# The reciprocal norm of layer 1's projections, multiplied by GpSimd and not by VectorE

## The chip, the cores and the metric

The program runs on one core of one Trainium2 chip. The metric is the device time of one execution in microseconds (us); the time of a kernel is the median of its runs. Engines are named as the profile names them: PE is TensorE, PEld its weight load, DVE is VectorE, ACT is ScalarE, POOL is GpSimd, SP is SyncE. Each runs its own list of instructions in order, and engines wait for one another through semaphores alone.

## What is computed

A two-layer trunk over 256 frames of width 2048, in float32. Layer 0 is attention beside a convolution module, layer 1 is a gated DeltaNet; behind each stands a SwiGLU feed-forward. The change lies in layer 1:

```python
def gated_deltanet_mixer(h, w_in, short_conv, a_log, dt_bias, o_norm, w_out):
    proj = h @ w_in                       # h is rms_norm(x, g): x * rsqrt(mean(x*x) + eps) * g
    qkv, z, b_logit, a_logit = jnp.split(proj, splits, axis=-1)
    qkv = jax.nn.silu(causal_depthwise_conv(qkv, short_conv))      # width 4
    q, k, v = jnp.split(qkv, [GDN_QK_WIDTH, 2 * GDN_QK_WIDTH], axis=-1)
    ...                                   # l2-normalise q and k, beta, log-decay g per head
    o = chunk_gated_delta_rule(q, k, v, g, beta)
    o = rms_norm(o, o_norm) * jax.nn.silu(zf)
    return o.reshape(bsz, seq, GDN_V_WIDTH).astype(h.dtype) @ w_out
```

The reciprocal norm of a frame is the same for all columns of the projection, so the kernel multiplies by it behind the matmul and not ahead of it.

## The kernel before

**Groups and chunks.** Every projection is cut into groups of 512 output columns, held transposed (128 columns on the partitions, 4 tiles of them, 256 frames along the row). A group goes through its 2048 input rows in 4 chunks `c`. SP loads a chunk of weights (1 MB) into `raw`; ACT rounds it into `w_hi` (L556, two halves), DVE makes the rest `w_lo` (L902, two halves), and PE multiplies both (L1664 and L1657) into the accumulators `acc`. At the end of a group ACT copies one half of `acc` into `tmp` (L563) and DVE adds the other (L908, 4 instructions) into `ut`; the last of the 4 gives the semaphore `acc_free` the value 4G+4, G being the number of the group.

**What follows a group.** A group is finished inside the next one, in `post`. DVE multiplies `ut` (128x1024) by `rstd`, the reciprocal norm (L967), and tells so by `scaled`. For a group of q, k or v DVE then runs the short convolution (L992, 4 instructions with one weight, then L994, 12 more), and ACT applies silu (L721). For a group of z, ACT applies silu to `ut` directly. The next group's sums on DVE wait until that silu has read `ut`.

**Segments of layer 1.** `in1_first` has the 4 groups q, k, v0, v1 of head set 0. `in1` runs three times; round j has z0 and z1 of set j and q, k, v0, v1 of set j+1, and beside them the delta rule of set j. `in1_last` has z0 and z1 of set 3, the delta rule of set 3 and 4 groups of the output projection (kind `resid`), whose inputs come back from DRAM (`og_save`). The multiplications at hand are those of the groups whose kind begins with gdn: 4 + 18 + 2 = 24.

**The delta rule** is a generator per engine (`gdn_pe`, `gdn_dve`, `gdn_act`, `gdn_pool`), advanced by ticks between the instructions of the groups; a tick lets it go on to the next `yield`, so the order on an engine is fixed when the program is built. POOL's part of set j, in its order: load `L` and `I` from `g_rows` (L1507), clear `XT`, add masks to `L` and `I` (L1512, L1514, 2 instructions each over 128x1024), clear `Xb` and `XTb`, then 8 small DMAs `l_diag` and 2 DMAs `Lb` (L1528, L1532), all inside the visit of z0; in the visit of q `x_diag` and `XT` (L1537, L1544); at the end of the round `og_save` (L1549) and a wait until it has landed. ACT needs the masks for its exponentials (L841), DVE needs `Lb` for an inversion of small triangles (L1419 to L1492), which keeps it busy through most of the group z1. The l2 norm of q and k is multiplied in by DVE at L1321, after the convolution of the v1 ahead has been started, and PE's first product of the delta rule (L1776) waits for it.

**In `in1_last`** POOL loads the first half of an old output back into `qk_in` (L532) at its visit of the first output group (b == 2), and the second half (L537) once two pieces of the first are used. ACT (L586) and DVE (L975) split them into `xs`, which PE needs for the group.

POOL comes to `post(before)` at the very start of a visit, ahead of the ticks of that visit:

```python
            def visit(here, before, kc):
                ...
                if before is not None:
                    post(before)
                ...
                if s.name == "in1_first" and b == 3:
                    ...                       # g_rows out, then wait until they have landed
                if s.deltanet:
                    if b == 0:
                        steps[0] = gdn_pool(pool, set_of(here))
                    if s.name == "in1_last" and b == 2:
                        ...                   # L532: qk_in<-og_save
```

Of the kernel before, what the change touches and what calls it, by code (L numbers as in the profile page):

```python
# [9 lines left out]
ALU = mybir.AluOpType  # L10
# [3 lines left out]
P = 128  # L14
T = 256
# [28 lines left out]
class Group:  # L44


    def __init__(self, w, col, rhs, kind, kc=4, row=0, step=0, at=0, norm=None):
        self.w, self.col, self.rhs, self.kind = w, col, rhs, kind
        self.kc, self.row, self.step, self.at, self.norm = kc, row, step, at, norm


class Segment:


    def __init__(self, name, n, groups, deltanet=False):
        self.name, self.n, self.groups = name, n, groups
        self.deltanet = deltanet
        self.scaled_of = [b for b, g in enumerate(groups) if g.kind != "resid"]
        self.conv_of = [b for b, g in enumerate(groups) if g.kind[:5] in ("gdn_q", "gdn_k", "gdn_v")]
        self.silu_of = [b for b, g in enumerate(groups) if g.kind.startswith("gdn")]  # L60

# [82 lines left out]
def trunk(nc, x, norm_mix0, w_in0, fgate_bias0, conv_w0, conv_b0, conv_ln_g0, conv_ln_b0, w_out0,  # L144
# [14 lines left out]
    with ctx:  # L159
# [28 lines left out]
        ut = sb("ut", [P, GM, T])  # L188
# [5 lines left out]
        rstd = sb("rstd", [P, T])  # L194
# [76 lines left out]
        def sem(name):  # L271
            return ctx.enter_context(nc.semaphore(name))
# [3 lines left out]
        acc_ready, tmp_ready, acc_free = sem("acc_ready"), sem("tmp_ready"), sem("acc_free")  # L276
# [27 lines left out]
        pool_mark, act_mark = sem("pool_mark"), sem("act_mark")  # L304
        fg_tmp, fox_lf = sem("fg_tmp"), sem("fox_lf")
        og_saved, og_back, scaled = sem("og_saved"), sem("og_back"), sem("scaled")
        og_hi, og_ready, sq_zeroed = sem("og_hi"), sem("og_ready"), sem("sq_zeroed")
        y_made, y_pe, y_out, out_sent = sem("y_made"), sem("y_pe"), sem("y_out"), sem("out_sent")

# [31 lines left out]
        def apart(pool):  # L341


            pool.sem_inc(pool_mark, 1)
# [67 lines left out]
        def pool_program(pool):  # L412
# [41 lines left out]
            def post(here):  # L454

                s, i, g, G = here.s, here.i, here.g, here.G
                if g.kind == "resid":
                    R = resid_no(here)
                    for m in range(GM):
                        pool.wait_ge(acc_free, 4 * G + m + 1)  # L460
                        apart(pool)
                        row = resid_row(here, m)
                        nc.gpsimd.tensor_tensor(row, row, ut[:, m], ALU.add).then_inc(resid_added, 1)  # L463
                    if g.norm is not None:

                        for m in range(GM):
                            n = 16 * g.norm + 4 * i + m
                            pool.wait_ge(resid_added, 4 * R + m + 1)
                            pool.wait_ge(sq_added, n)
                            apart(pool)  # L470
                            row = resid_row(here, m)
                            nc.gpsimd.tensor_tensor(sq_one[:], row, row, ALU.mult).then_inc(sq_made, 1)  # L472
                            pool.wait_ge(sq_made, n + 1)
                            nc.gpsimd.tensor_tensor(sq_acc[:], sq_acc[:], sq_one[:], ALU.add).then_inc(sq_added, 1)  # L474
                if g.kind == "glu_gate":

                    pool.wait_ge(glu_sig, i + 1)
                    nc.gpsimd.tensor_tensor(u_pad[:, 4 * i:4 * i + 4, CONV_W - 1:], gt[:], ut[:],
                                            ALU.mult).then_inc(glu_made, 1)
                if g.kind == "up":  # L480

                    q = s.pair + i
                    pool.wait_ge(gate_silu, q + 1)
                    pool.wait_ge(scaled, here.scaled + 1)
                    nc.gpsimd.tensor_tensor(ut[:], gt[:], ut[:], ALU.mult).then_inc(h_prod, 1)  # L485
                    pool.wait_ge(h_prod, q + 1)
                    apart(pool)
                    hb = hs[g.at % 2]
                    hi = hb[:, bass.ds(4 * i, 4), 0, :]
                    nc.gpsimd.tensor_copy(hi, ut[:]).then_inc(h_hi, 1)  # L490
                    pool.wait_ge(h_hi, q + 1)
                    apart(pool)
                    nc.gpsimd.tensor_tensor(hb[:, bass.ds(4 * i, 4), 1, :], ut[:], hi.bitcast(F32),  # L493
                                            ALU.subtract).then_inc(h_ready, 1)
# [205 lines left out]
        def silu_act(act, here):  # L700

            kind = here.g.kind
            if here.b in here.s.conv_of:
                act.wait_ge(sc_step, 8 * here.conv + 8)
            else:
                act.wait_ge(scaled, here.scaled + 1)
            if here.s.name == "in1" and kind == "gdn_q":
                all_heads(act, gd_pe, NP * here.i + P_KQ)
            if here.s.name == "in1" and kind == "gdn_k":
                all_heads(act, gd_pe, NP * here.i + P_Z6)  # L710
            if here.s.name == "in1" and kind == "gdn_v0":
                all_heads(act, gd_pe, NP * here.i + P_O)
            if kind == "gdn_z0":
                if isinstance(here.i, int) and here.i == 0 and here.s.name == "in1":
                    act.wait_ge(rows_out, 32)
                else:
                    act.wait_ge(og_saved, 16 * set_of(here))
            dst = {"gdn_q": qk_in[:, 0], "gdn_k": qk_in[:, 1], "gdn_v0": vs[:, 0:4], "gdn_v1": vs[:, 4:8],
                   "gdn_z0": zs[:, 0:4], "gdn_z1": zs[:, 4:8]}[kind]
            src = gt if here.b in here.s.conv_of else ut  # L720
            nc.scalar.activation(dst, src[:], ACT.Silu).then_inc(conv_silu, 1)  # L721
# [175 lines left out]
        def vector_program(dve):  # L897
# [57 lines left out]
            def post(here):  # L955


                g = here.g
                if g.kind == "resid":
                    if g.norm in (1, 2, 3):  # L960
                        dve.wait_ge(resid_added, 4 * resid_no(here) + 4)
                        dve.wait_ge(xs_ready, 4 * g.norm + here.i)
                        gain_split(g.norm, here.i)
                    return
                dve.wait_ge(acc_free, 4 * here.G + 4)
                dst = place(here)
                nc.vector.tensor_tensor(dst, dst, rstd[:].unsqueeze(1).to_broadcast([P, 4, T]), ALU.mult)\  # L967
                    .then_inc(scaled, 1)
# [9 lines left out]
            def conv_step_of(here, q):  # L978
# [3 lines left out]
                i, b = here.i, here.b - here.s.conv_of[0]  # L982
                j = i + 1 if here.s.name == "in1" else 0
                ct = (4 * j, 16 + 4 * j, 32 + 8 * j, 36 + 8 * j)[b]
                if s:
                    dve.wait_ge(sc_step, 2 * n0 + q - 1)
                else:
                    dve.wait_ge(scaled, here.scaled + 1)
                for m in range(2 * (q % 2), 2 * (q % 2) + 2):
                    w = short_w[:, 3 - s, bass.ds(ct + m, 1)]  # L990
                    if s == 0:
# [76 lines left out]
            here = walk(dve, visit)  # L1068
# [909 lines left out]
```

## Time and profile before

| | before |
|---|---|
| median of 3 runs | 3061.31 us (3058.98 to 3062.45) |
| profiled execution, its own time | 3066.37 us |
| its span in the trace | 3064.6 us |
| mean granted TensorE clock | 0.954 |
| PE busy | 2823.5 us (92%) |
| DVE busy | 1953.2 us (64%) |
| ACT busy | 1402.8 us (46%) |
| POOL busy | 641.6 us (21%) |

Times in the trace are counted from the start of the span, so they run to 3064.6; the execution's own time is 1.8 us longer. Layer 1's mixer lies between 1270 and 2240 us. The rounds of `in1` begin at about 1376, 1577 and 1785 us, `in1_last` at 1993.

### The profile page before, as it was taken

The page shows a single profiled execution, that of the slowest core. Times are in us where ns is not written, and L with a number is a line of the kernel's source. Part 1 is how long each engine was busy: PE and PEld are TensorE (multiplying, and loading weights), DVE is VectorE, ACT ScalarE, POOL GpSimd, SP SyncE. Part 2 cuts the span into 40 slices and gives each one's busy share as a digit, 9 for nine tenths or more (in the row PEclk, how much of TensorE's full clock was granted, in tenths as well). Part 3 has the DMA queues.
Part 4 walks back from the last instruction along what each step waited for, and adds up shares of the span by engine and source line. Part 5 has one row for each costly group of instructions (what it writes and reads, how often), then busy time and mean ns, then how long its engine had stood idle before and what let it go on. Part 6 is the DMA issues. An engine that isn't in the chain of part 4 may idle for free. (4 is left out here: it accounts for less than half of the span.)

```text
span 3064.6 us, 43790 instructions
## 1 busy us (share of the span) xinstructions
PE 2823.5 (92%) x15973; PEld 2468.6 (81%) x15973; DVE 1953.2 (64%) x2454; ACT 1402.8 (46%) x2142; POOL 641.6 (21%) x549
## 2 busy tenths in 40 slices
PE   6966889999999999999888988979899999999997
PEld 5855668888888888877777877868788888888886
DVE  4599547555555555687768668677466555555655
ACT  3455434444444444456355453463444444444443
POOL 4054014111110113321021020031142101110214
PEclk8988879999999999999999999999999999999999
DMA  5533225555555555554444355354455555555553
GB/s 170 165 110 110 97 69 180 191 191 193 179 192 190 192 184 177 168 193 135 131 165 152 119 174 154 124 189 144 138 185 185 188 193 183 190 192 189 182 177 110
DMA packets 246088, 502.26 MB, mean 164 GB/s; under 512 B 10919, under 2 KB 11528, under 8 KB 244392
## 3 DMA queue, kind: packets, MB, share of 16 engines
q1 hardware_dynamic: 237232, 473.99, 47.2%
q0 software_dynamic: 5888, 25.79, 2.4%
q8 instruction: 97, 1.59, 0.2%
q10 hardware_dynamic: 2808, 0.38, 0.1%
q14 instruction: 63, 0.52, 0.0%
HBM read 491.64 MB, written 8.49 MB: 163 GB/s over the span
## 5 line engine op out<-in xcount | busy, mean ns | idle before, releaser
L902 DVE TENSOR_TENSOR w_lo<-raw,w_hi 128x1024 fp32r<-128x1024 f32 (+1 forms) x912 | 1168.8, 1315 | 789.0 <-ACT w_hi L556 788.1
L1664 PE MATMUL acc<-xs,w_hi 128*128 128x512 f32 x5248 | 1337.2, 403 | 59.9 <-ACT w_hi L556 27.1
L556 ACT ACTIVATE w_hi<-raw 128x1024 fp32r<-128x1024 f32 (+1 forms) x912 | 905.5, 1036 | 934.8 <-PE acc L1657 927.7
L1664 PEld LDWEIGHTS acc<-xs,w_hi 128*128 128x128 f32 x5248 | 981.7, 194 | 254.0 <-issue 43.9
L1657 PE MATMUL acc<-xs,w_lo 128*128 128x256 f32 x5248 | 720.2, 288 | 68.9 <-DVE w_lo L902 68.9
L1657 PEld LDWEIGHTS acc<-xs,w_lo 128*128 128x128 f32 x5248 | 693.7, 194 | 104.9 <-DVE w_lo L902 75.1
L1664 PE MATMUL acc<-hs,w_hi 128*128 128x512 f32 x1920 | 468.2, 393 | 15.5 <-issue 11.5
L1664 PEld LDWEIGHTS acc<-hs,w_hi 128*128 128x128 f32 x1920 | 351.8, 189 | 83.2 <-issue 13.1
L563 ACT ACTIVATE tmp<-acc 128x256 f32<-128x256 f32 x456 | 172.8, 383 | 358.0 <-PE acc L1657 307.6
L1657 PEld LDWEIGHTS acc<-hs,w_lo 128*128 128x128 f32 x1920 | 251.4, 191 | 12.6
L1657 PE MATMUL acc<-hs,w_lo 128*128 128x256 f32 x1920 | 255.3, 282 | 0.0
L485 POOL TENSOR_TENSOR ut<-gt,ut 128x1024 f32<-128x1024 f32 x22 | 52.9, 2404 | 837.8 <-DVE ut L967 837.8
L908 DVE TENSOR_TENSOR ut<-acc,tmp 128x256 f32<-128x256 f32 x336 | 135.0, 420 | 135.9 <-ACT tmp L563 132.0
L463 POOL TENSOR_TENSOR xT<-xT,ut 128x256 f32 (+1 forms) x140 | 103.1, 759 | 496.9 <-DVE ut L908 496.8
L1219 DVE SCALAR_TENSOR_TENSOR conv<-u_pad,conv_w,conv 128x256 f32<-128x256 f32 x120 | 100.3, 900 | 0.0
L994 DVE SCALAR_TENSOR_TENSOR gt<-ut,short_w,gt 128x255 f32<-128x255 f32 (+2 forms) x192 | 94.7, 551 | 0.2
L1255 POOL TENSOR_TENSOR conv<-conv,prod 128x1024 f32<-128x1024 f32 x30 | 80.1, 2671 | 62.8 <-ACT prod L1244 56.3
L474 POOL TENSOR_TENSOR sq_acc<-sq_acc,sq_one 128x256 f32<-128x256 f32 x60 | 68.8, 1147 | 4.7
L493 POOL TENSOR_TENSOR hs<-ut,hs 128x1024 f32 (+1 forms) x22 | 68.3, 3103 | 5.3 <-POOL hs L490 5.3
L1549 POOL DMA_DIRECT2D og_save<-zs x4 | 3.7, 915 | 296.4 <-DVE zs L1398 296.4
L472 POOL TENSOR_TENSOR sq_one<-xT 128x256 f32 (+1 forms) x60 | 63.7, 1061 | 7.6 <-POOL sq_acc L474 4.1
L908 DVE TENSOR_TENSOR gt<-acc,tmp 128x256 f32<-128x256 f32 x96 | 38.4, 420 | 34.5 <-ACT tmp L563 33.2
(290 smaller groups left out, 1655.0 us busy)
## 6 DMA issues: line engine op xcount, KB each, us to landing
raw<-in_w_in SPq DMA_DIRECT2D x136, 1024.0 KB, 5.2
raw<-in_w_gate SPq DMA_DIRECT2D x88, 1024.0 KB, 5.1
raw<-in_w_up SPq DMA_DIRECT2D x88, 1024.0 KB, 5.1
raw<-in_w_down SPq DMA_DIRECT2D x64, 1024.0 KB, 5.1
raw<-in_w_out SPq DMA_DIRECT2D x48, 1024.0 KB, 5.1
raw<-in_w_down SPq DMA_DIRECT2D x32, 768.0 KB, 4.4
L<-g_rows POOLq DMA_DIRECT2D x4, 1536.0 KB, 8.3
I<-g_rows POOLq DMA_DIRECT2D x4, 1536.0 KB, 12.5
```

The source lines that it names most:

```text
L463: nc.gpsimd.tensor_tensor(row, row, ut[:, m], ALU.add).then_inc(resid_added, 1)
L474: nc.gpsimd.tensor_tensor(sq_acc[:], sq_acc[:], sq_one[:], ALU.add).then_inc(sq_added, 1)
L493: nc.gpsimd.tensor_tensor(hb[:, bass.ds(4 * i, 4), 1, :], ut[:], hi.bitcast(F32), ALU.subtract).then_inc(h_ready, 1)
L556: nc.scalar.activation(w_hi[:, c % 2, k], raw[:, c, k], ACT.Copy).then_inc(hi_ready, 1)
L563: nc.scalar.activation(tmp[:, m % 2], acc[:, m, T:2 * T], ACT.Copy).then_inc(tmp_ready, 1)
L902: nc.vector.tensor_tensor(w_lo[:, c % 2, k], raw[:, c, k], w_hi[:, c % 2, k].bitcast(F32), ALU.subtract).then_inc(lo_ready, 1)
L908: nc.vector.tensor_tensor(dst, acc[:, m, 0:T], tmp[:, m % 2], ALU.add).then_inc(acc_free, 1)
L994: last = nc.vector.scalar_tensor_tensor(gt[:, m, s:T], ut[:, m, 0:T - s], w, gt[:, m, s:T], ALU.mult, ALU.add)
L1219: return eng.scalar_tensor_tensor(conv[:, ct], u_pad[:, ct, k:k + T], w, conv[:, ct], ALU.mult, ALU.add)
L1255: nc.gpsimd.tensor_tensor(conv[:, CONV_DVE:], conv[:, CONV_DVE:], prod[:, k % 2], ALU.add)\
L1657: last = mm(acc[:, m, T:2 * T], w_lo[:, c % 2, k, cols], r[:, kk, 0], start=False, stop=end, skip_group_check=True)
L1664: mm(acc[:, m, :], w_hi[:, c % 2, k, cols], r[:, kk], start=kk == 0, stop=end, skip_group_check=True)
```

## The change

The 24 multiplications leave DVE's list and enter POOL's, in `post`, each with a wait for the group's 4 sums. A semaphore `gdn_scaled` tells of them; the first convolution instructions of DVE and the silu of a z group on ACT wait for it in place of `scaled`. The groups of the other kinds are multiplied by DVE as before.

```diff
-        self.scaled_of = [b for b, g in enumerate(groups) if g.kind != "resid"]
+        self.scaled_of = [b for b, g in enumerate(groups) if g.kind != "resid" and g.kind[:3] != "gdn"]
...
+        gdn_scaled = sem("gdn_scaled")
...
                 # pool_program, post(here), after the branch for "glu_gate"
+                if g.kind.startswith("gdn"):
+                    pool.wait_ge(acc_free, 4 * G + 4)
+                    nc.gpsimd.tensor_tensor(ut[:], ut[:], rstd[:].unsqueeze(1).to_broadcast([P, 4, T]), ALU.mult)\
+                        .then_inc(gdn_scaled, 1)
...
                 # silu_act
             else:
-                act.wait_ge(scaled, here.scaled + 1)
+                act.wait_ge(gdn_scaled, here.silu + 1)
...
                 # vector_program, post(here)
+                if g.kind.startswith("gdn"):
+                    return
                 dve.wait_ge(acc_free, 4 * here.G + 4)
...
                 # conv_step_of
-                    dve.wait_ge(scaled, here.scaled + 1)
+                    dve.wait_ge(gdn_scaled, here.silu + 1)
```

The list of POOL at the end of `in1_first` and the start of the first round of `in1` stands here as it was, without times:

```order
L521 DMA g_rows<-row_l 32x384
L523 DMA g_rows<-row_i 32x384
L1507 DMA L<-g_rows 128x3072
L1507 DMA I<-g_rows 128x3072
L1509 MEMSET XT 128x2048
L1512 TENSOR_TENSOR L<-L,mask_fox 128x8x128 x2
```

The same place in the changed kernel, where line 483 is the new multiplication and the other lines have moved down by 5 to 7:

```order
L483 TENSOR_TENSOR ut<-ut,rstd 128x1024 x3
L526 DMA g_rows<-row_l 32x384
L528 DMA g_rows<-row_i 32x384
L483 TENSOR_TENSOR ut<-ut,rstd 128x1024
L1514 DMA L<-g_rows 128x3072
L1514 DMA I<-g_rows 128x3072
```

Three multiplications (q, k, v0) now stand ahead of the rows' way out, and that of v1 stands between it and the loads of `L` and `I`. In every later round it is also the multiplication of v1 that stands ahead of these loads.

In `in1_last` POOL's list before runs from the last DMAs of the visit of z0 straight to the reload:

```order
L1528 DMA l_diag<-L 32x8x32 x8
L1532 DMA Lb<-l_diag 64x1024 x2
L532 DMA qk_in<-og_save 128x8x256
L537 DMA qk_in<-og_save 128x8x256
L1537 DMA x_diag<-XTb 64x256 x2
```

And in the changed kernel:

```order
L1535 DMA l_diag<-L 32x8x32 x8
L1539 DMA Lb<-l_diag 64x1024 x2
L483 TENSOR_TENSOR ut<-ut,rstd 128x1024 x2
L537 DMA qk_in<-og_save 128x8x256
L542 DMA qk_in<-og_save 128x8x256
```

The multiplications of z0 and z1, each behind the sums of its group, stand ahead of the first reload of `qk_in`.

## Rows read from the trace of the kernel before

**Rows 1.** Windows: us, then busy us of each engine, PEclk, DMA share, GB/s

```profile
1577.00:1785.00 208.00, 182.40 (x1070) 159.19 (x1069) 152.68 (x241) 101.12 (x186) 29.05 (x29) 0.94 0.45 149
600.00:800.00 200.00, 200.00 (x1151) 176.56 (x1150) 117.46 (x117) 89.38 (x112) 36.17 (x15) 1.00 0.58 188
```

**Rows 2.** Waits of 1577 to 1785: total us, times, longest us

```profile
PE aux L1776 <- DVE qk_in L1321: 8.6, 1, 8.6
PE acc L1657 <- DVE w_lo L902: 7.6, 2, 5.6
PE aux L1805 <- DVE X L1360: 2.7, 1, 2.7
```

**Rows 3.** Line L967: duration ns min/median/max, first and last start

```profile
L967 DVE TENSOR_TENSOR ut<-ut,rstd x48: 1214/1218/1221, 65.6 to 2886.6; 128x1024 f32<-128x1024 f32 x48
```

**Rows 4.** Line L485, POOL's product in the feed-forward, same columns

```profile
L485 POOL TENSOR_TENSOR ut<-gt,ut x22: 2395/2405/2410, 567.7 to 2888.0; 128x1024 f32<-128x1024 f32 x22
```

**Rows 5.** Timeline of POOL in layer 1: start us, us, instruction, idle before it

```profile
1338.09 0.56 POOL L1507 DMA_DIRECT2D L<-g_rows  x1 [4.10 <-DMA g_rows<-row_i]
...
1352.44 6.30 POOL L1512 TENSOR_TENSOR L<-L,mask_fox 128x1024 f32<-128x1024 f32 x2 [11.43 <-DMA I<-g_rows]
...
1590.95 5.69 POOL L1512 TENSOR_TENSOR L<-L,mask_fox 128x1024 f32<-128x1024 f32 x2 [9.82 <-DMA I<-g_rows]
1596.60 5.85 POOL L1514 TENSOR_TENSOR I<-I,mask_up 128x1024 f32<-128x1024 f32 x2
...
1892.71 1.29 POOL L1544 DMA_DIRECT2D XT<-x_diag  x2 [0.72 <-issue]
...
2050.53 0.92 POOL L532 DMA_DIRECT2D qk_in<-og_save  x1
2070.64 0.90 POOL L537 DMA_DIRECT2D qk_in<-og_save  x1 [19.18 <-DVE xs L975]
```

**Rows 6.** Timeline of DVE in layer 1, same columns

```profile
1375.19 0.76 DVE L908 TENSOR_TENSOR ut<-acc,tmp 128x256 f32<-128x256 f32 x2 [0.18 <-ACT tmp L563]
...
1390.74 2.36 DVE L902 TENSOR_TENSOR w_lo<-raw,w_hi 128x1024 fp32r<-128x1024 f32 x2 [7.99 <-ACT w_hi L556]
1393.02 3.24 DVE L994 SCALAR_TENSOR_TENSOR gt<-ut,short_w,gt 128x255 f32<-128x255 f32 x8
...
1591.38 6.35 DVE L902 TENSOR_TENSOR w_lo<-raw,w_hi 128x1024 fp32r<-128x1024 f32 x2 [7.07 <-ACT w_hi L556]
1597.64 7.46 DVE L994 SCALAR_TENSOR_TENSOR gt<-ut,short_w,gt 128x255 f32<-128x255 f32 x8
...
1651.66 0.68 DVE L1437 TENSOR_TENSOR prod<-XTb,Lb 128x512 f32<-128x512 f32 x1
...
1894.35 1.14 DVE L992 TENSOR_SCALAR gt<-ut,short_w 128x256 f32<-128x256 f32 x4 [0.19 <-DVE ut L967]
...
2066.13 0.74 DVE L908 TENSOR_TENSOR ut<-acc,tmp 128x256 f32<-128x256 f32 x2
...
2067.99 2.35 DVE L975 TENSOR_TENSOR xs<-qk_in,xs 128x1024 fp32r<-128x1024 f32 x2
```

**Rows 7.** Timeline of PE in layer 1, same columns

```profile
1368.40 2.07 PE L1657 MATMUL acc<-xs,w_lo 128*128 128x256 f32 x8 [4.70 <-DVE w_lo L902]
...
1399.72 0.49 PE L1776 MATMUL aux<-qk_in 128*128 128x128 f32 x2 [0.58 <-DVE qk_in L1321]
...
1608.56 0.80 PE L1776 MATMUL aux<-qk_in 128*128 128x128 f32 x2 [8.61 <-DVE qk_in L1321]
...
2069.31 6.40 PE L1664 MATMUL acc<-xs,w_hi 128*128 128x512 f32 x16 [5.55 <-issue]
...
2096.01 2.08 PE L1657 MATMUL acc<-xs,w_lo 128*128 128x256 f32 x8 [2.96 <-DVE w_lo L902]
```

**Rows 8.** Timeline of ACT in `in1_last`, same columns

```profile
2064.18 1.99 ACT L586 ACTIVATE xs<-qk_in 128x1024 fp32r<-128x1024 f32 x2
```

**Rows 9.** Tile `qk_in`, 2000 to 2200: its two loads from DRAM

```profile
DMA to landing us min/median/max: 6.0/8.5/10.9
```

## The prediction

> **What bounds the kernel now.** I read the windows first [rows 1]. In the feed-forward of layer 0 PE is busy for all of 200 us. In a round of layer 1 (1577 to 1785) it is busy for 182.4 of 208 us: 25.6 us are lost to waits. DVE, at 152.7 us, is the busiest of the others and POOL, at 29.1, is nearly idle. So far the change looks right. But a share of busy time doesn't say which instruction PE waits for. The waits of that round do [rows 2]: once 8.6 us for the l2-normalised keys (L1321), twice together 7.6 us for `w_lo`, 2.7 us for the transposes of `X`. I then laid the timelines of DVE, POOL and PE beside each other around these waits. What matters is what DVE does just ahead of each.
>
> **What leaves DVE.** 24 multiplications of 1.22 us [rows 3], 29.3 us. Behind most of them DVE comes to stand anyway: in the start of a round it waits 7 to 8 us for ACT's `w_hi` after the multiplication of v1 (idle of 7.99 and 7.07 ahead of L902 [rows 6]). A saved 1.22 us only lengthens such a wait, worth nothing. It counts in one stretch per round: the inversion during z1, where DVE runs without a gap until `w_lo` comes, for which PE waits.
>
> **What POOL pays.** The nearest row is its product of the same shape, also in place on `ut`: 2.40 us [rows 4]. The new one repeats one operand over the tiles; the mask additions, which repeat an operand too, take 2.85 and 2.93 us each (5.69 and 5.85 for two [rows 5]). I take 2.4 and keep 2.9 for the range. POOL's own time is no bound: 24 x 2.4 = 58 us more in 870.
>
> **What POOL's work does to DVE.** Two `w_lo` take 2.36 us alone (1390.74) and 6.35 us beside the masks (1591.38); 8 convolution steps take 3.24 us alone and 7.46 us partly beside them [rows 6]. The masks ended at 1602.45 [rows 5], so 2.65 of these 7.46 us were free and held 6 steps at 0.40 us; the other 4.81 us held 2, about 2.4 us each. So an instruction of DVE with two inputs in SBUF runs at 0.37 of its speed, a convolution step at 0.17, as long as POOL adds or multiplies.
>
> **Term 1, the masks of the first set: -4.7 and +8.0.** Before, `L` and `I` of set 0 were loaded at 1338.09, during v1 of `in1_first`, and the masks ran beside it from 1352.44 on [rows 5]; PE then waited 4.70 us for a `w_lo` [rows 7]. Now the sums of v0 and the multiplication stand ahead of the rows' way out, and those of v1 ahead of the load. The 4 sums of v1 end at 1375.95 [rows 6]; plus 2.4 is 1378.4, plus the 14.4 us that lay between load and mask (1338.09 to 1352.44) is 1392.7, or 1391 if the loads wait 9.82 and not 11.43 us for their data, as in the next round. The first DVE work of that start begins at 1390.74. So the masks now fall on the very instructions that they fell on in the next round, whose price stands there: PE waits 8.61 us where it waited 0.58 [rows 7]. That is +8.0 (+6 if they start early, +9.5 if late), and the wait of 4.70 goes, -4.7.
>
> **Term 2, the masks of sets 1 to 3: +3.9.** The multiplication of v1 stands ahead of these loads as well, so the masks come 2.4 us later, from 1593.35 to 1604.85 in the second round. DVE starts at 1591.38: 1.97 us of its two `w_lo` (2.36 us) are free, the rest takes 1.1, so it is through at 1594.4; until 1604.85 it makes 4.3 steps at 2.4, the remaining 3.7 take 1.5: 1606.4, where the row ended at 1605.10. +1.3 for each of three starts; 0 to 2.4 each in the range, 2.4 being all that a load can come later.
>
> **Term 3, the inversion: -0.7.** The multiplication of z1 leaves DVE's gapless stretch, 1.22 us. On POOL it starts with the last sum of z1, at 1651.7, in that same stretch. The instruction that begins then (L1437, 0.68 us [rows 6]) has two inputs in SBUF and pays about 0.9 us by the rate above; those behind it read PSUM or are reductions, for which these rows show no price. 0.2 to 0.3 gained, in three rounds: -0.7; the ends are +0.7 and -3.4.
> The Trainium skill (SBUF — State Buffer, "Who interferes with whom") has the port pair that DVE and GpSimd share as a lock held for a whole instruction, taken by whoever starts first, and says that reductions and single SBUF inputs don't contend. DVE would start first here and pay nothing, and the sum would be 2.7 us lower; the masks' rows agree that the slow-down is no even sharing. The rule speaks against the change: it moves work from one side of a shared port to the other.
>
> **Term 4, q: +1.6.** In the third round POOL issues its last `XT` DMAs until 1894.00 [rows 5]. Only then can it multiply q, until 1896.4, and DVE's first convolution instruction started at 1894.35 [rows 6]: 2.1 us late, of which I let 0.5 vanish in DVE's next wait. The transposes of `X`, for which PE waits, stand behind it. In the other rounds POOL should be free in time; 0 to 4 for all.
> The multiplications of z0 should be done about 1 us before ACT asks; those of k, v0 and the first three I cost at nothing: DVE makes two `w_lo` beside them, loses about what it saves, and PE has `w_lo` in hand. Without this cover each costs up to 1.2.
>
> **Term 5, the reload of `qk_in`: +7.3.** It was issued at 2050.53, while z1 was still being multiplied by PE, and lay ready when ACT came to it at 2064.18 [rows 5, 8]. Now the multiplication of z1 stands ahead of it, which waits for the last sum, at 2066.87 [rows 6]. The product ends at 2069.3, and the load needs 6.0 to 10.9 us [rows 9]. I take 6.0, since the second load, issued at 2070.64, was the quick one (DVE used it behind other work, and no `w_lo` is made while DVE stands still, so no weights are loaded beside). Landed at 2075.3, first ACT copy (half of 1.99 us [rows 8]) done at 2076.4: DVE starts L975 at 2076.5 and not 2067.99 [rows 6], 8.5 us late, and everything queued behind it, the inversion too. PE, which began at 2069.31, just after the first of the two L975, is as late. DVE then makes up 1.2, the multiplication of z1, before the wait of PE at 2096.01 [rows 7]. 8.5 - 1.2 = 7.3; with 10.9 it is 12.2.
>
> **The sum**: -4.7 + 8.0 + 3.9 - 0.7 + 1.6 + 7.3 = 15.4, say 15 us. The profiled execution took 3066.37 us, 1.8 more than its span and 5.1 more than the median, so it becomes 3081; the median of 3061.3 becomes 3076.3, +0.5%.
>
> **Rivals.**
> *The reload takes long*: 10.9 us as its first load did, +20, 3081. For it: the longer time is that of this very load. Against it: `L`, `Lb` and weights moved then, and they don't now. 0.14.
> *The sides balance*: the masks of set 0 come early enough to collide less, the later starts cost nothing, the lock rule holds in the inversion. -4.7 + 6 - 3.4 + 7.3 = +5, 3066; with q free of charge and part of the reload hidden, under the 6 us that a measurement of this kernel can tell from no change (0.2%). 0.13.
> *Faster, by DVE's relief*: the three waits for DVE in a round [rows 2] each shorten by the 1.2 us ahead of them, 3.6 in four rounds, -14.4; with -4.7, the reload's +7.3 and q's +1.6 that is -10, 3051. It decides if the multiplication lies on DVE's path into each wait and POOL's masks don't. Against it: the idle of 7 us between them. 0.06.
> *No effect at all* would need a multiplication that POOL hides everywhere; the order of the reload excludes it.
> The forecast has 0.67.
>
> **The numbers.** Lower end: -4.7 + 6 + 0 - 3.4 + 0 + 7.3 = +5, 3066. Upper end: -4.7 + 9.5 + 7.2 + 0.7 + 4 + 12.2 = +29, all at their worst at once; the likeliest case and the slow reload with two terms at their upper ends reach +24, so 3085. Slower by over 0.2%: 0.67 + 0.14 = 0.81, within 0.13, faster 0.06.
>
> **What would show it.** Term 1: the masks of set 0 near 1391 less the 4.7 us gained, PE's wait near 1368 gone and one of 8 us or more at the first L1776. Term 2: the other waits at L1776 about a microsecond longer. Term 3: DVE's stretch in z1 as long as before, not 1.2 us shorter. Term 4: DVE's first convolution instruction of q in the third round waiting for POOL. Term 5: the first `qk_in` load behind the sums of z1, and PE idle some 14 us in place of 5.55. I am wrong if that gap stays near 6 us, if masks no longer slow DVE, or if the new product takes far longer than 2.4 us.

## The result

The changed kernel takes 3070.81 us in the median (3067.41 to 3073.08, 8 runs); the kernel before took 3062.23 on the same chip (3058.68 to 3064.19, 8 runs). The ratio of the two is put at 1.0026 [1.0017, 1.0035]: 8.0 us more, 5.2 to 10.7 by the interval (the two medians themselves lie 8.6 apart). That is slower, and within the range, and about half of the 15 us forecast.

The profiled execution of after took 3067.41 us, its span is 3065.9. The one of before happened to be 4 us above its median and the one of after 3 us below, so the two traces differ by 1.3 us in span alone, and a total says nothing here: trace must be laid beside trace place by place. The page of after begins with the busy times (us, share, instructions):

```profile
PE 2814.2 (92%) x15973; PEld 2461.7 (80%) x15973; DVE 1947.8 (64%) x2430; ACT 1403.4 (46%) x2142; POOL 701.6 (23%) x573
```

DVE has given up 24 instructions of 1.22 us, 29.3 us, and its busy time fell by 5.4: its other instructions became 24 us longer. POOL has 60 us more, for 24 products of 2.46 us on average. The window of the second round, columns as in [rows 1]:

```profile
1577.00:1785.00 208.00, 182.76 (x1065) 159.89 (x1064) 145.99 (x232) 96.55 (x183) 42.78 (x36) 0.93 0.45 147
```

PE is idle for 25.2 us of this window, where it was 25.6. What it waited for in the three rounds (1376 to 1993) is another matter. The view of waits, total us, times, longest, first of before:

```profile
PE acc L1657 <- DVE w_lo L902: 21.3, 6, 5.6
PE aux L1776 <- DVE qk_in L1321: 12.8, 3, 8.6
PE acc L1664 <- DVE ut L908: 8.9, 8, 2.4
PE aux L1805 <- DVE X L1360: 8.1, 3, 2.7
...
PE aux L1860 <- DVE L L1331: 4.2, 3, 3.1
```

and of after, where the lines stand 5 to 7 lower:

```profile
PE aux L1783 <- DVE qk_in L1328: 22.0, 3, 9.1
PE acc L1664 <- DVE w_lo L907: 20.1, 6, 5.5
PE aux L1812 <- DVE X L1367: 11.0, 3, 4.1
...
PE acc L1671 <- DVE ut L913: 4.6, 6, 2.3
...
PE aux L1867 <- DVE L L1338: 1.8, 3, 0.8
```

Two waits grew, for `qk_in` by 9.2 and for `X` by 2.9. Three shrank, for `ut` by 4.3, for `w_lo` by 1.2 and for `L` (L1860 before, L1867 now) by 2.4.

To place the loss I took, from DVE's timeline, the end of the fourth sum of every group; from one group to the next is a step. Up to v0 of `in1_first`, and for v0 and v1 of a round, and for the third and fourth output group, the steps are the same in both kernels but for 0.4 us. The others, means of two executions of each kernel (a second one of each is the first experiment below), in us:

| step | before | after | difference |
|---|---|---|---|
| v1 of `in1_first` | 29.9 | 22.3 | -7.6 |
| z0, first round | 38.0 | 44.3 | +6.3 |
| z0, second and third round, and in `in1_last` | 132.3 | 133.8 | +1.5 |
| z1 + q, three rounds, and z1 in `in1_last` | 217.2 | 209.4 | -7.7 |
| k, three rounds | 99.9 | 105.5 | +5.6 |
| two output groups | 66.3 | 73.7 | +7.4 |
| layer 1's mixer and the step behind it | 977.2 | 982.3 | +5.2 |

Ahead of layer 1 both kernels run the same code, and its time alone varies from 1256.4 to 1258.6 us in these four traces; and the last row itself is 980.5 in one trace of after and 984.2 in the other. So 5.2 by the traces and 8.0 by the medians don't contradict each other.

### The profile page after: what moved, and what is told of

It reads as the page before. It is cut to its first block and busy times, and to the rows that moved or that the text cites. A ratio compares the mean times of both kernels' runs of the same rounds, so it can differ in the third digit from the quotient of the medians.

```text
span 3065.9 us, 43797 instructions
## 1 busy us (share of the span) xinstructions
PE 2814.2 (92%) x15973; PEld 2461.7 (80%) x15973; DVE 1947.8 (64%) x2430; ACT 1403.4 (46%) x2142; POOL 701.6 (23%) x573
## 5 line engine op out<-in xcount | busy, mean ns | idle before, releaser
L907 DVE TENSOR_TENSOR w_lo<-raw,w_hi 128x1024 fp32r<-128x1024 f32 (+1 forms) x912 | 1191.0, 1340 | 792.4 <-ACT w_hi L561 791.4
L483 POOL TENSOR_TENSOR ut<-ut,rstd 128x1024 f32<-128x1024 f32 x24 | 59.1, 2462 | 355.7 <-DVE ut L913 348.5
L913 DVE TENSOR_TENSOR gt<-acc,tmp 128x256 f32<-128x256 f32 x96 | 38.4, 421 | 34.5 <-ACT tmp L568 33.2
```

Of the source, the lines that this page charges most:

```text
L907: nc.vector.tensor_tensor(w_lo[:, c % 2, k], raw[:, c, k], w_hi[:, c % 2, k].bitcast(F32), ALU.subtract).then_inc(lo_ready, 1)
L913: nc.vector.tensor_tensor(dst, acc[:, m, 0:T], tmp[:, m % 2], ALU.add).then_inc(acc_free, 1)
```

## The profile after, term by term

**The first set (term 1).** POOL's timeline at the end of `in1_first`, columns as in [rows 5]:

```profile
1366.23 2.40 POOL L483 TENSOR_TENSOR ut<-ut,rstd 128x1024 f32<-128x1024 f32 x1 [18.98 <-DVE ut L913]
1368.59 0.59 POOL L1514 DMA_DIRECT2D L<-g_rows  x1
...
1380.20 5.67 POOL L1519 TENSOR_TENSOR L<-L,mask_fox 128x1024 f32<-128x1024 f32 x2 [8.67 <-DMA I<-g_rows]
1385.85 5.85 POOL L1521 TENSOR_TENSOR I<-I,mask_up 128x1024 f32<-128x1024 f32 x2
```

The load now stands behind the product of v1, and the masks (1380.20 to 1391.70) fall on the first DVE work of the round:

```profile
1380.85 6.11 DVE L907 TENSOR_TENSOR w_lo<-raw,w_hi 128x1024 fp32r<-128x1024 f32 x2 [8.39 <-ACT w_hi L561]
1386.89 7.46 DVE L1001 SCALAR_TENSOR_TENSOR gt<-ut,short_w,gt 128x255 f32<-128x255 f32 x8
```

6.11 and 7.46 us: the 6.35 and 7.46 of [rows 6] a round later. On PE's timeline the old wait is gone, and its place has a new one:

```profile
1361.28 1.12 PE L1664 MATMUL acc<-xs,w_lo 128*128 128x256 f32 x8
...
1397.81 0.80 PE L1783 MATMUL aux<-qk_in 128*128 128x128 f32 x2 [8.54 <-DVE qk_in L1328]
...
1406.80 0.70 PE L1867 MATMUL aux<-qk_in 128*128 128x256 f32 x2 [0.32 <-DVE L L1338]
```

The last of these lines is what the forecast lacked. Before, PE waited there too:

```profile
1408.70 0.89 PE L1860 MATMUL aux<-qk_in 128*128 128x256 f32 x2 [3.05 <-DVE L L1331]
```

The new wait of 8.54 us swallows that of 3.05 behind it.

**The inversion (term 3)**: DVE and then POOL at the end of z1's sums:

```profile
1645.97 0.68 DVE L1444 TENSOR_TENSOR prod<-XTb,Lb 128x512 f32<-128x512 f32 x1
1646.57 0.69 DVE L1357 TENSOR_TENSOR vb<-aux,gate_b 128x512 f32<-128x512 f32 x1
1647.17 1.21 DVE L1449 TENSOR_REDUCE sq_one<-prod 128x128 f32<-128x1024 f32 x1
```

```profile
1646.13 2.78 POOL L483 TENSOR_TENSOR ut<-ut,rstd 128x1024 f32<-128x1024 f32 x1 [14.15 <-DVE ut L913]
```

DVE was first by 0.16 us and kept its 0.68 us; POOL's product took 2.78 us, not 2.40. An instruction that reads PSUM, and a reduction, are as long beside the product as without it.

**q (term 4)**: POOL and then DVE in the second round:

```profile
1676.47 2.61 POOL L1551 DMA_DIRECT2D XT<-x_diag  x4 [2.63 <-DMA x_diag<-XTb]
1679.10 2.42 POOL L483 TENSOR_TENSOR ut<-ut,rstd 128x1024 f32<-128x1024 f32 x1
```

```profile
1681.71 1.14 DVE L999 TENSOR_SCALAR gt<-ut,short_w 128x256 f32<-128x256 f32 x4 [2.75 <-POOL ut L483]
```

The sums of q ended at 1676.08 (1675.18 and 0.90 us). The product starts 3.0 us later, behind the four `XT` DMAs, and DVE waits 2.75 us for it.

**The reload (term 5)**: POOL, then ACT, then PE:

```profile
2061.40 2.72 POOL L483 TENSOR_TENSOR ut<-ut,rstd 128x1024 f32<-128x1024 f32 x1 [13.65 <-DVE ut L913]
2064.07 0.95 POOL L537 DMA_DIRECT2D qk_in<-og_save  x1
```

```profile
2070.11 2.00 ACT L591 ACTIVATE xs<-qk_in 128x1024 fp32r<-128x1024 f32 x2 [10.65 <-DMA qk_in<-og_save]
```

```profile
2072.52 5.54 PE L1671 MATMUL acc<-xs,w_hi 128*128 128x512 f32 x16 [13.05 <-issue]
```

Issue to use 6.0 us, PE idle 13.05 us where it was idle 5.55 [rows 7].

## The experiments

Rivals after the result: that the reload's place costs 7 us and the masks' place most of the rest (my theory), or that the loss is DVE's slowdown by POOL's 58 us of products all over the layer, in which case moving DMAs would bring little. Each variant ran against before on its own chip. Where it is set against after, the two ratios to before are subtracted (after: 1.0026), and a thousandth is 3.06 us. One ratio has an interval of about 0.0009 to either side, which is 2.8 us; the difference of two is uncertain by about 4 us.

**1. A second look at each kernel**, unchanged.

> The changed kernel once more, unaltered, for a second trace. The two traces in hand differ by 1.2 us in span, the medians by 8.6 us, so one of them must hold something that not every execution has. If the steps of the groups of layer 1 are a matter of order alone, they come again within 0.5 us (the group of v1 in in1_first 7.6 us shorter than before, z0 of the first round 6.4 longer, the first output group 4.9 and the second 2.1 longer), and the difference of executions lies outside layer 1's mixer. Rival: they are a matter of when the loads of L and I land, and the starts of the rounds differ by 1 us or more from trace to trace.

> The kernel before once more, unaltered. Theory of order: its groups in layer 1's mixer take the same time as in the first trace within 0.5 us. Rival: the starts of the rounds (37 to 44 us for z0) differ by 1 us or more.

3073.22 and 3066.16 us. The steps of v0 and v1, and those of z0, come again within 0.6 us but for one of 1.0 (z0 in `in1_last`). The expectation of 0.5 us everywhere failed for the others: z1, q and k differ by up to 2 us between two executions of one kernel, and the first output group of before took 36.7 us once and 34.0 the other time. Differences of this size in those steps say little in a single trace; where one is read below, it is from several traces.

**2. The reload, both ways.** In the changed kernel, the first reload put ahead of the product of z1 (its old place, further down, is taken out):

```diff
+                if s.name == "in1_last" and b == 2:
+                    all_heads(pool, gd_pe, NP * (SETS - 1) + P_KQ)
+                    pool.dma_start(qk_in[:]..., og_rows(0)).then_inc(og_back, 16)
                 if before is not None:
                     post(before)
```

and in the kernel before, with the products on DVE, the same reload made to wait for the sums of z1:

```diff
                     if s.name == "in1_last" and b == 2:
                         all_heads(pool, gd_pe, NP * (SETS - 1) + P_KQ)
+                        pool.wait_ge(acc_free, 4 * here.G)
                         pool.dma_start(qk_in[:]..., og_rows(0)).then_inc(og_back, 16)
```

> The changed kernel with the first reload of qk_in issued ahead of the multiplication of z1 in in1_last. If the reload behind z1 costs what the traces show (first and second output group 7.0 us longer), the time falls by 7 us and a bit more, since the 1.2 us that DVE saves in the inversion then stand alone: -7 to -8.5, to the time of before or 1 us above. Rival: the idle time of PE there has another cause (the multiplication, or the clock), and less than 3 us come back.

> The kernel before, with one wait added: POOL issues the first reload of qk_in only when the sums of z1 are done. No multiplication is moved. By the forecast's term 5 without the 2.4 us of the product and without DVE's relief: load issued at 2066.9, landed 6.0 us later, first L975 at 2074.0 and not 2068.0, so +6.0 us against before. Rival: the time comes from POOL's product and not from the order of the load; then within 1 us of before.

The first: 3063.7 us (3058.42 to 3068.47), ratio to before 1.0005 [0.9996, 1.0014], so 6.4 less than after, a little short of the 7 to 8.5 expected; its two output groups take 66.2 us again. The second: 3070.11 (3065.45 to 3073.92), ratio 1.0021 [1.0012, 1.003], +6.4, where 6.0 was expected; the groups take 72.2. Both DMAs in the trace, first of the one, then of the other, and PE's idle time behind each:

```profile
2046.76 2.42 POOL L483 TENSOR_TENSOR ut<-ut,rstd 128x1024 f32<-128x1024 f32 x1
2049.10 0.95 POOL L510 DMA_DIRECT2D qk_in<-og_save  x1
```

```profile
2067.76 5.24 PE L1670 MATMUL acc<-xs,w_hi 128*128 128x512 f32 x16 [6.87 <-issue]
```

```profile
2061.16 0.91 POOL L533 DMA_DIRECT2D qk_in<-og_save  x1 [17.02 <-DVE ut L909]
```

```profile
2069.71 6.12 PE L1665 MATMUL acc<-xs,w_hi 128*128 128x512 f32 x16 [12.20 <-issue]
```

So the wait alone, without any multiplication moved, gives the loss, and the place alone takes it away. These 6.4 us (7.4 in the steps) are an order on a queue; whether the 2.7 us of the product ahead of the load add to them is below what two such runs can tell.

**3. The masks of the first set.** In the changed kernel, the rows' way out goes ahead of the product of v0, and the loads of `L` and `I` of set 0 ahead of that of v1:

```diff
+                if s.name == "in1_first" and b == 3:
+                    ...                       # g_rows out, wait until landed
+                ahead = s.name == "in1" and here.starts
+                if ahead:
+                    steps[0] = gdn_pool(pool, set_of(here))
+                    next(steps[0])            # up to a new yield behind the loads
                 if before is not None:
                     post(before)
```

> The changed kernel, in which POOL sends the rows of set 0 ahead of the multiplication of v0 and loads L and I of set 0 ahead of that of v1; the masks stay behind it. The loads then land during v1, and the masks of set 0 begin as soon as v1 is multiplied, about 2.4 us behind its sums, and last some 10.4 us, over before DVE begins the 2 w_lo and 8 convolution steps ahead of L1321. Theory (the price of the first start is the masks beside DVE's instructions): PE's wait of 8.5 us at the first L1783 falls under 2 us, 6 to 8 us less than the changed kernel, that is about the time of before. Rival: the price comes from the longer way of the loads, which also fetch 3 MB; then masks placed early save less than 2 us.

3063.21 us (3058.84 to 3067.32), ratio 1.0003 [0.9994, 1.0012], so 7.0 less than after. z0 of the first round takes 36.4 us, where after has 44.3 and before 38.0; v1 stays at 22.3. The masks now lie 11 us earlier, POOL and then DVE:

```profile
1369.10 6.65 POOL L1525 TENSOR_TENSOR L<-L,mask_fox 128x1024 f32<-128x1024 f32 x2
```

```profile
1373.44 7.54 DVE L1004 TENSOR_SCALAR gt<-ut,short_w 128x256 f32<-128x256 f32 x4
1381.43 2.36 DVE L912 TENSOR_TENSOR w_lo<-raw,w_hi 128x1024 fp32r<-128x1024 f32 x2 [0.45 <-ACT w_hi L566]
```

They slow DVE there too: four first convolution steps take 7.54 us, for 1.14 alone. But behind them DVE waited 8.39 us in after for `w_hi`, and that wait shrinks to 0.45. The masks cost nothing here because DVE has the time, not because DVE is left alone.

**4. Both, and in every round.** All loads ahead of the products of their visit, and the reload as well (the two diffs above, with `ahead` in every visit of z0):

> The changed kernel with all of POOL's loads ahead of its multiplications: the rows and loads of set 0, L and I of every round, and the reload of qk_in. Against the changed kernel: -7 for the reload, -6 to -8 for set 0, and -1.3 for the three other starts, which lie 1.5 to 2 us earlier than in the changed kernel. Sum -14 to -16, so 6 to 8 us faster than before. Rival: the multiplication on POOL costs by itself, beside DVE and in front of the convolution of q; then no faster than before.

3053.85 us (3052.14 to 3056.72), ratio 0.9974 [0.9965, 0.9984]: faster than before by 8.0, as expected. With all 24 products still on POOL the kernel gains; the rival, by which POOL's products themselves are the loss, falls with it.

But these 8.0 us are not DVE's relief alone. By the steps this kernel is 10.1 us shorter than before, and 7.6 of them are v1 of `in1_first` (22.3 us for 29.9). There the masks of set 0 used to run beside DVE's work from 1352.44 on [rows 5]; now they stand behind the product of v1 and start at 1371.37. That is once more a place in POOL's queue. The other steps come to -2.5: z1 and q gain 6.3, k loses 4.3. The kernel before with nothing but these masks moved was not run; it may have most of the gain without any product moved.

**5. q.** The changed kernel with the products of q left on DVE:

```diff
-                if g.kind.startswith("gdn"):
+                if g.kind.startswith("gdn") and g.kind != "gdn_q":
```

> The changed kernel with the multiplications of q alone back on DVE; the other 20 stay on POOL. In the trace of the changed kernel DVE waits 2.75 us for POOL's q in the second round, since POOL issues the XT loads first, and the group behind it is 0.7, 2.1 and 1.0 us longer than before. Theory: these 3.8 us come back less up to 1.2 us of DVE's own work in each of three rounds: -1 to -3.8. Rival: POOL's q is hidden behind DVE's wait for w_hi, and nothing changes, within 1 us.

3067.18 us (3062.22 to 3069.93), ratio 1.0014 [1.0005, 1.0023]: 3.7 less than after, which the medians alone can't tell from nothing. The steps bear it out: the three of k are back at 33.1 us each, from 35.2 on average in the two traces of after. Over all fourteen traces, 13 of the 15 steps of k with q on POOL take 35.1 to 35.8 us (two take 33.6 and 33.7), and of the 27 with q on DVE 20 take 33.1 and seven 34.5 to 34.7. PE's wait for `X`, 1376 to 1993:

```profile
PE aux L1817 <- DVE X L1372: 8.1, 3, 2.7
```

It is the 8.1 us of before.

**6. z1 alone.** Only the products of z1 on POOL, the reload ahead of them, twice with the same kernel (the condition in `post`; the reload is moved as in 2):

```diff
+                if g.kind == "gdn_z1":
```

> Only the 4 multiplications of z1 are on POOL, and the reload of qk_in is ahead of the last one; the other 20 are on DVE, and every load of POOL stands where it stood before. If the relief of DVE in its gapless stretch is whole, as the trace of the changed kernel shows (L1444 keeps its 0.68 us and POOL takes 2.78 in place of 2.40), each round gains 1.2 us: -4.8 against before, at least -3. By the forecast's rate (0.9 us paid by DVE each time) it is -1.2.

> The kernel with only z1 on POOL once more, unaltered: its median was 1.6 us under before, its trace (the fastest of its executions) 10 us under. If z1's relief is whole in every execution, as z1 and q of each round show in that trace (62.2 to 59.1, 62.5 to 60.0, 61.1 to 60.3), the median is 3 to 5 us under before and the first measurement lay at its edge. By the forecast's rate it is 1.2 under.

3060.43 us (3055.53 to 3062.87), ratio 0.9995 [0.9985, 1.0004], and 3059.93 (3055.59 to 3063.45), ratio 0.9993 [0.9984, 1.0002]: -1.5 and -2.1 us. I had expected -4.8 from the traces. The intervals reach from +1.2 to -4.6 us and from +0.6 to -4.9, so by the medians the gain is not even told from nothing. The traces of the two show z1 + q shorter by 0.5 to 3.1 us a round.

All fourteen traces together say more. From the last sum of z1 to DVE's last copies of the inversion (L1492 before) it is 24.7 us in every round of the four traces with z1 on DVE, and 23.5 in every round of the ten with z1 on POOL. So DVE gains 1.1 us in each of three rounds, and in `in1_last` nothing (29.6 us with the reload in its place, 29.2 before). The steps of z1 and q, the table's row, are 213.6 to 218.5 us in the four and 208.0 to 212.7 in the ten, 5.5 apart in the mean. How much of that arrives in the total stays open.

**7. The masks of `I` behind the normalised keys.** If PE's wait at L1776 is what the masks cost, moving the two of `I` behind that point should free DVE. In the kernel before:

```diff
-            for n, mask in ((0, mask_up), (2, mask_up)):
-                nc.gpsimd.tensor_tensor(I[:, :, n], ...)
...                                            # POOL's wait for L1321
+            for n, mask in ((0, mask_up), (2, mask_up)):
+                nc.gpsimd.tensor_tensor(I[:, :, n], ...)
```

> The kernel before, with the two mask additions to I (5.85 us of POOL) moved behind POOL's wait for L1321; those to L stay where they were. Nothing of the change is in it. Theory: the waits for L1321 (8.6 us and alike) are DVE's instructions beside the masks, so with half the masks gone from there DVE makes its convolution steps at 0.40 in place of 2.4 us and PE's wait at L1776 falls by 4 to 5 us in the second round and in1_last, by 1 or 2 in the third, where less of it lay beside them, and by none in the first: -8 to -12. Rival: ACT's exponentials of I or the DMAs of l_diag behind them become late, and the time comes back within the same group: within 3 us.

3069.42 us (3065.88 to 3071.6), ratio 1.0017 [1.0008, 1.0026]: 5 us slower, where 8 to 12 faster was expected. PE's waits in the three rounds:

```profile
PE aux L1860 <- DVE L L1331: 20.5, 3, 7.4
...
PE aux L1776 <- DVE qk_in L1321: 7.1, 3, 4.4
```

The wait for `qk_in` fell by 5.7 us as meant, and the next one rose by 16.3. DVE in the second round, then POOL, then ACT, tell why:

```profile
1605.23 5.90 DVE L994 SCALAR_TENSOR_TENSOR gt<-ut,short_w,gt 128x253 f32<-128x253 f32 x4
```

```profile
1604.36 5.70 POOL L1516 TENSOR_TENSOR I<-I,mask_up 128x1024 f32<-128x1024 f32 x2 [7.82 <-DVE qk_in L1321]
```

```profile
1611.16 1.06 ACT L721 ACTIVATE vs<-gt 128x1024 f32<-128x1024 f32 x1 [11.70 <-DVE gt L994]
...
1614.48 0.40 ACT L841 ACTIVATE L<-L,gate_c 128x128 f32<-128x128 f32 x1
```

The masks now lie on the last four convolution steps, which take 5.90 us (the same four took 1.65 before, with no mask beside them). The silu of v1 waits for them and starts where it did before (at 1611.24 there), the exponentials of `L` stand behind that silu on ACT, and PE's products of L1860 behind those. PE comes to them at the same time as before, but after a longer wait; first this kernel, then before:

```profile
1617.55 1.22 PE L1860 MATMUL aux<-qk_in 128*128 128x256 f32 x2 [5.78 <-DVE L L1331]
```

```profile
1617.64 0.70 PE L1860 MATMUL aux<-qk_in 128*128 128x256 f32 x2 [0.63 <-DVE L L1331]
```

The granted clock just behind is 0.50 (1.2 GHz), where it was 1.00, and z0 of this round takes 46.1 us for 44.1. The start of a round is held by convolution, silu, `L`; the wait at L1776 was only where PE came to stand first. That is the 3.05 us that vanished in term 1, seen from the other side. In the first round, where masks and convolution had not met, z0 goes from 38.0 to 44.5, and in the third from 44.1 to 48.6. What is gained is in v1 of `in1_first`, with only the masks of `L` beside it: 25.6 us for 29.9.

**8. The best of the parts**, loads and reload ahead (4) with q on DVE (5), and the same with the late masks of `I` (7):

> All loads ahead of the multiplications as in the kernel that is 8 us faster than before, and the 4 multiplications of q on DVE. The two parts lie in different groups, so their gains add: -8 and -3.5, about -11.5 against before (3050.5). Rival: DVE's wait for POOL's q was already gone with the earlier loads; then within 1 us of 3053.9.

> The same, with the masks of I behind the wait for L1321 as well. If the masks beside DVE are what the starts of the rounds cost, this takes off what the other run of this call with the late masks takes off before: -8 to -12 more, 3039 to 3043. In the first round, where all masks now lie ahead of DVE's instructions, nothing. Rival: the masks of I then delay the chain behind them, and it gains less than 3.

3052.23 us (3048.67 to 3053.65, 5 runs), ratio 0.9962 [0.9948, 0.9976]: 11.6 us faster than before, as expected (11.5), and the fastest of all, though not proven faster than 4 (0.9974, the intervals overlap). With the late masks 3061.9 (3058.07 to 3064.87), ratio 0.9998 [0.9989, 1.0007]: they take back nearly all of it, as in 7, where the expectation had 8 to 12 more to gain.

## Why the prediction was right, and where its sizes were off

The direction, the reason for it (places in POOL's queue, not POOL's time) and the range held. The sum was 15.4 us; the steps give 5.5 and the medians 8.0 (5.2 to 10.7). So the range held near its lower end, +5, and of the five terms only the reload came out as costed. It alone about makes up the loss; the others, forecast at +8.1 together, come to -1.9 in the steps.

**Term 1, -4.7 and +8.0, measured -7.6 and +6.3.** The masks came at 1380.20. I had them at 1392.7 less the 4.7 gained, 1388.0; the step of v1 gave 2.9 us more, the lag from load to mask was 11.6 and not 14.4, and the feed-forward ahead happened to be 1.9 us shorter in this execution. They hit the instructions forecast, and the wait was 8.54 for 8.61. What failed is that I took one wait of PE for the whole step. In before, behind the wait of 4.70 [rows 7], PE's timeline goes on

```profile
1370.27 2.60 PE L1664 MATMUL acc<-xs,w_hi 128*128 128x512 f32 x8
...
1374.82 3.91 PE L1664 MATMUL acc<-xs,w_hi 128*128 128x512 f32 x16 [1.00 <-DVE ut L908]
```

so a wait of 1.00 us follows, and the matmuls behind the first wait run at the lower clock level: 2.07 us for 8 [rows 7] and 2.60, where after has

```profile
1362.23 2.00 PE L1671 MATMUL acc<-xs,w_hi 128*128 128x512 f32 x8
```

and 1.12 for the 8 ahead of it. The granted clock from 1368.40 to 1370.30 is 0.50, and 1.00 in after from 1361.28 to 1364.30. 4.70 + 1.00 + 0.95 + 0.60 = 7.25 of the 7.6. And of the 8.0 new us, 2.7 were had back at L1860 (3.05 to 0.32). So the term changed its sign: +3.3 forecast, -1.3 measured. Experiment 3 shows its second half: without the collision 7.0 us less. Experiment 7 shows the first: with half of the masks gone from v1, its step falls by 4.3.

**Term 2, +3.9, measured +1.5 in the steps.** I let the masks come 2.4 us later, the length of a product. But the load of `L` before waited for the landing of `og_save`, and that goes on while the product runs. In before POOL's timeline of the second round has

```profile
1570.34 0.92 POOL L1549 DMA_DIRECT2D og_save<-zs  x1 [91.87 <-DVE zs L1398]
1578.14 0.57 POOL L1507 DMA_DIRECT2D L<-g_rows  x1 [6.88 <-issue]
```

where the sums of v1 had ended at 1577.2; after issues it at 1574.26, 2.4 us behind its sums (which end at 1571.83), so only 1.5 us later against them. Taken to the start of the masks it is 1.2, 1.6 and 0 us for sets 1 to 3.

**Term 3, -0.7; measured with term 4 only.** z1 and q together gained 7.7 us in the traces, and the wait for `ut` fell by 4.3. I had said that DVE's stretch in z1 would stay as long. From the start of L1437 to the last copy of the inversion (L1492, at 1676.19 before) it was 24.5 us; after, from 1645.97 to 1669.36, 23.4: 1.1 us shorter, nearly the whole product, and so in every trace (experiment 6). The step that failed is the 0.9 us I charged to L1437: it began before POOL's product and paid nothing. (By the forecast's own rate the charge would have been 1.2: 0.68 / 0.37 is 1.84.) That is the forecast's alternative of -3.4. The Trainium skill's rule (SBUF — State Buffer, "Who interferes with whom"), a lock held for an instruction by whoever is first, and no contention for reductions, agrees with this place of the trace: 0.68 us for DVE's instruction, 2.78 for POOL's, 1.21 for the reduction. How much of the 7.7 us is real is open, since experiment 6 found 2 us in its medians.

The rate itself is not what the traces show. DVE and then POOL in the second round of after:

```profile
1749.24 2.74 DVE L907 TENSOR_TENSOR w_lo<-raw,w_hi 128x1024 fp32r<-128x1024 f32 x1 [0.80 <-ACT w_hi L561]
```

```profile
1748.52 2.38 POOL L483 TENSOR_TENSOR ut<-ut,rstd 128x1024 f32<-128x1024 f32 x1 [34.77 <-DVE ut L913]
```

The product ends at 1750.90 and `w_lo` 1.08 us behind it. So it is with all 13 `w_lo` of this trace that started while a product had 0.2 us or more to run: they end 1.08 or 1.09 us behind it (they take 1.22 alone), however long it still had. DVE didn't run at 0.37 of its speed; it stood still until POOL's instruction was done, as the rule's lock has it. But the part of the rule on who is first doesn't always hold: the `w_lo` that started at 1471.77, 0.4 us ahead of a product, took 3.90 us, and the product its usual 2.40 (term 4); ten more are alike in the other traces. Nor were single SBUF inputs free, as the prediction put it: the first convolution steps took 7.54 us for 1.14 in experiment 3. The Trainium skill excepts DVE's 2-port modes in the same section, and no run here shows whether these steps ran in one.

**Term 4, +1.6, measured +5.6 in the steps of k, 3.7 (give or take 4) by experiment 5.** I had POOL late in the third round alone and free in time in the others. It had no margin there. In before's second round POOL's timeline has

```profile
1682.99 2.61 POOL L1544 DMA_DIRECT2D XT<-x_diag  x4 [2.37 <-DMA x_diag<-XTb]
```

until 1685.60, 1.75 us behind q's last sum (1683.85). Plus 2.4 for the product is 4.2 us behind it, and DVE's convolution started at just that (1688.05). Now it starts 5.6 us behind the sum; 0.6 of the delay vanish in DVE's next wait, much as I had it, and `X` is transposed 0.9 us later. In the first round DVE doesn't wait for the product but works beside it, and that is no cheaper; DVE and then POOL:

```profile
1470.63 5.04 DVE L907 TENSOR_TENSOR w_lo<-raw,w_hi 128x1024 fp32r<-128x1024 f32 x2 [0.52 <-ACT w_hi L561]
```

```profile
1472.18 2.40 POOL L483 TENSOR_TENSOR ut<-ut,rstd 128x1024 f32<-128x1024 f32 x1
```

5.04 us for 2.36. So the term was due three times and not once, 2.9 us of waits for `X`; that the steps of k grew by more than these waits is shown and not explained.

**Term 5, +7.3, measured +7.4** by the steps, 6.4 each by undoing it and by doing it alone. The load took the quick 6.0 us that I had chosen, PE's gap was 13.05 for "some 14".

**Together**: term 1 was too high by 4.6, term 2 by 2.4, terms 3 and 4 by 3.0 in sum, term 5 too low by 0.1: 15.4 - 9.9 = 5.5, the sum of the steps. Of the rivals, *the sides balance* (+5 us) was nearer to the 8.0 measured than the forecast's 15.4, and its 0.13 too little: it had DVE's whole relief in the inversion and nearly free later starts in it. By the 5.5 us of the steps the result would be this rival's, which ended under 6 us; that the medians put it into the forecast's share is partly luck. *The reload takes long* and *faster, by DVE's relief* are excluded as results of this change. Of the second, the 1.1 us a round in the inversion were there; the 14.4 us it reckoned with are shown by no run, and the largest part of the gain of experiment 4 is another thing, the masks of set 0 out of v1.

## What to carry to other kernels

When work moves to an engine that also issues DMAs, first list the DMAs that now stand behind the wait of that work: here the places of one reload and of the first set's loads cost some 13 us against the same kernel with them put first. Look also for what becomes faster by the same shift: masks that left one place of collision brought 7.6 us, and none of it is relief of the engine that gave up the work. A wait of PE's is not the size of a step: a new one swallows the waits behind it, a removed one takes the lower clock behind it along, so ask which chain ends last (here convolution, silu, `L`) and not only where PE stands. Elementwise work of POOL was cheap where DVE had a wait behind it or read PSUM, and elsewhere stretched DVE's instructions to two to six times their length, so choose its place in time.

## What the runs showed of the hardware

- A `w_lo` of DVE that started well inside POOL's product ended 1.08 or 1.09 us behind the product's end, in all 13 cases of after: it waited for POOL's instruction and was not merely slower. POOL kept its 2.4 us.
- Who starts first doesn't settle who waits: DVE's L1444, 0.16 us ahead of the product, took 0.68 us as ever and the product 2.78 for 2.40; the `w_lo` at 1471.77, 0.4 us ahead of one, took 3.90 for 1.22 and the product 2.40. Which property decides is open.
- Beside POOL's masks four convolution steps with two tensor inputs took 5.90 us for 1.65, and four with one tensor input (L1004 in experiment 3) 7.54 for 1.14.
- DVE's reduction (1.21 us) and its multiplication from PSUM (0.69 us) had the same length beside POOL's product as without.
- A wait costs PE more than its length: the matmuls behind the 4.70 us ran at the lower clock level (1.2 GHz, granted 0.50) first, 2.07 us for what took 1.12.
